# Convolution layer and pooling layer in one block, with the pooling done by banded matrices on TensorE

## What is computed

```
# odd layer (h = modulated RMS norm of x)
bg, cg, xt, g = split(h @ odd_w_in, 4)            # 1024 -> 4 x 1024
conv = three-tap convolution of cg * xt along positions
x = x + gate * ((bg * conv * silu(g)) @ odd_w_out)

# pooling layer
h = x * rsqrt(mean(x*x, channels) + eps) * norm_mix_g
for each of 4 groups of 256 channels, windows w = 2, 4, 8, 16:
    d = (mean of the last w positions of h, fewer at the start) - h
    y = d @ pool_w[group] + pool_b                # 256 x 256 per group
x = x + pool_scale * y
```

## Time and profile before

| quantity | value |
|---|---|
| time, median of 3 runs | 2083.51 us (2082.96 to 2085.34) |
| span of the profiled execution | 2083.1 us |
| TensorE matmul busy | 1915.1 us, 92% |
| VectorE busy | 1061.5 us, 51% |
| ScalarE busy | 621.8 us, 30% |
| GpSimd busy | 474.6 us, 23% |
| mean HBM traffic | 60 GB/s |

### The profile page before, as it was taken

The page is one execution under the profiler, slowest core; times in us unless marked ns, Lnnn a source line. Parts: engine busy times, 40 slices in busy tenths (PEclk is TensorE's granted clock), DMA queues, the critical chain, the costliest instruction groups (busy, mean ns, idle before and its releaser), DMA issues. The chain is left out here.

```text
span 2083.1 us, 24691 instructions
## 1 busy us (share of the span) xinstructions
PE 1915.1 (92%) x9917; PEld 1611.9 (77%) x9917; DVE 1061.5 (51%) x1007; ACT 621.8 (30%) x815; POOL 474.6 (23%) x200
## 2 busy tenths in 40 slices
PE   5799999889996989999999964699999999999998
PEld 3799988668885867888888853578888888888886
DVE  3633662468886325333333379744544535445454
ACT  4312211556665213222212032422222222222222
POOL 0211211000000212322222126222323233232221
PEclk9899999999998989999999986799999999999999
DMA  7311112800001412111111000111102111020212
GB/s 289 128 41 41 48 51 66 334 23 1 0 0 61 162 35 57 51 51 51 50 50 50 10 21 0 51 59 32 60 30 60 39 52 60 30 60 30 60 40 81
DMA packets 132701, 125.90 MB, mean 60 GB/s; under 512 B 6510, under 2 KB 118695, under 8 KB 131495
## 3 DMA queue, kind: packets, MB, share of 16 engines
q1 hardware_dynamic: 132647, 125.12, 18.8%
HBM read 113.57 MB, written 11.53 MB: 60 GB/s over the span
## 5 line engine op out<-in xcount | busy, mean ns | idle before, releaser
L2009 DVE TENSOR_TENSOR residual<-ps,residual 128x1024 f32<-128x1024 f32 x176 | 215.1, 1224 | 199.5 <-PE ps L106 199.2
L628 PE MATMUL ps<-in_hi,h_hi 128*128 128x256 f32 x512 | 145.7, 285 | 9.1 <-DVE h_lo L194 9.1
L628 PE MATMUL ps<-in_lo,h_hi 128*128 128x256 f32 x512 | 145.5, 284 | 0.0
L628 PE MATMUL ps<-in_hi,h_lo 128*128 128x256 f32 x512 | 145.5, 284 | 0.0
L1931 ACT ACTIVATE branches<-ps,cols 128x1024 f32<-128x1024 f32 x44 | 53.1, 1207 | 271.4 <-PE ps L106 264.8
L1994 DVE SCALAR_TENSOR_TENSOR branches<-ps,cols,branches 128x1023 f32<-128x1023 f32 x44 | 56.2, 1278 | 141.7 <-ACT branches L1931 141.7
L122 POOL TENSOR_TENSOR in_lo<-in_raw,in_hi 128x2048 fp32r<-128x2048 f32 (+1 forms) x16 | 59.4, 3715 | 287.2 <-ACT in_hi L119 233.7
L1647 DVE SCALAR_TENSOR_TENSOR residual<-ps,ada_col,residual 128x1024 f32<-128x1024 f32 x64 | 81.6, 1282 | 81.6 <-PE ps L106 77.5
L106 PE MATMUL ps<-yf_hi,f_hi 128*128 128x512 f32 x336 | 105.8, 396 | 1.1 <-DVE residual L2009 1.1
L106 PE MATMUL ps<-h_hi,hi_va 128*128 128x512 f32 x336 | 104.3, 392 | 2.6 <-DVE branches L1997 2.6
L628 PEld LDWEIGHTS ps<-in_hi,h_hi 128*128 128x128 f32 x512 | 99.0, 193 | 9.5 <-issue 9.5
(11 more groups left out here) (354 smaller groups left out, 4398.7 us busy)
## 6 DMA issues: line engine op xcount, KB each, us to landing
ada_raw_rest<-in_ada_w SPq DMA_DIRECT2D x32, 512.0 KB, 6.1
raw_va<-in_ffn_w_in SPq DMA_DIRECT2D x22, 512.0 KB, 5.5
raw_ga<-in_ffn_w_in SPq DMA_DIRECT2D x22, 512.0 KB, 6.4
f_raw<-in_ffn_w_out SPq DMA_DIRECT2D x22, 512.0 KB, 3.6
ada_raw<-in_ada_w SPq DMA_DIRECT2D x8, 1024.0 KB, 18.9
in_raw<-in_even_w_in SPq DMA_DIRECT2D x8, 1024.0 KB, 5.2
residual<-in_x SPq DMA_DIRECT2D x2, 2048.0 KB, 10.7
x_scratch<-fq SPq DMA_DIRECT2D x8, 512.0 KB, 6.1
```

Source lines behind the costliest of these rows:

```text
L628: last = pe.matmul(ps[:, n % 8, 0:HALF_GROUP], x[:, k, r * P:(r + 1) * P], w[:, u % 2, k, :], start=(k == 0 and x is hi and w is w_hi), st ...
L2009: dve.tensor_tensor(res[:, d, :], pair[DOWN_PAIR[d]], res[:, d, :], ALU.add)\
```

## The change

The block `pool` is gone, and its work stands in the block `odd`. It uses that the norm is one number per position and the projection runs over channels, so the two can be exchanged.

- **Weights.** `norm_mix_g` is multiplied into the pooling weights (`pool_weights`, ScalarE). They are loaded into the buffers `raw_cg` and `raw_xt` of the odd layer once those are free, and split as before.
- **Projection of the raw residual.** `res` tiles are split into `h1_hi` and `h1_lo` when they are final (`high`, `x_low`). `z_group(r, g)` then makes the rows of position block r, group g: six products of 256 columns, where the x tile is the stationary operand, so that the result lies with positions on partitions. Position blocks 0 to 2 run ahead of the mean of squares, blocks 3 to 7 behind it.
- **Norm.** The square sum stands in the odd block. Its root and reciprocal are applied as one scale per partition when the result is copied out of PSUM (`z_high` on ScalarE, `z_low` on VectorE). The eight transposes (L210) of the pooling layer are gone.
- **Pooling.** `banded(m)` multiplies each position block of z with a matrix of 128 by 144 that holds window mean minus identity. Per channel tile m there are 16 products of 144 or 128 columns and three of 16. The matrices are made by VectorE (`window_ones`, before the first step of the odd layer) and GpSimd (`bands`, after the last one).
- **End.** `pool_add`, bias and the square sum for the ffn norm are as before, with other buffers.

```diff
+                        def z_group(r, g):
+                            out = pair[Z_PAIR[r % 4]][:, g * HALF_GROUP:(g + 1) * HALF_GROUP]
+                            for t in (2 * g, 2 * g + 1):
+                                for x, w in ((h1_hi, hi), (h1_hi, lo), (h1_lo, hi)):
+                                    last = pe.matmul(out, x[:, t, r * P:(r + 1) * P], pool_weight(w, t),
...
+                        def banded(m):
+                            g, out, cs = m // 2, pair[Z_PAIR[m % 4]], slice(m * P, (m + 1) * P)
+                            for b in range(RT):
+                                if m == 0:
+                                    pe.wait_ge(sem("z_low"), b + 1)
...
                         down(N - 1, N, (last_d_hi, last_d_lo, last_y_hi, last_y_lo))
-                        squares.tensor(pe)
...
+                        pe.wait_ge(sem("pw_low"), 2)
+                        for g in range(4):
+                            x_low_stands(pe, 2 * g)
+                            x_low_stands(pe, 2 * g + 1)
+                            for r in range(3):
+                                if g == 0 and r:
+                                    res_final(pe, 4 + r)
+                                last = z_group(r, g)
...
+                        for p, (name, tiles) in enumerate((("x_summed_pool", SUM_ON_POOL), ("x_summed_dve", SUM_ON_VECTOR))):
+                            pe.wait_ge(sem(name), len(tiles))
...
+                        for r in range(3, RT):
+                            if r == 3:
+                                pe.wait_ge(sem("x_rooted"), 1)
+                            else:
+                                pe.wait_ge(sem("z_low"), r - 3)
...
+                        for m in range(KT):
+                            if m >= 4:
+                                pe.wait_ge(sem("pool_added"), m - 3)
+                            else:
+                                pe.wait_ge(sem("z_low"), 5 + m)
+                            banded(m)
                         squares.tensor(pe)
```

More of the change, by code:

```diff
@@ L1597, in _ @@
                         last_rest()
-                        for d in squares.ON_POOL:
-                            squares.add(pool, d)
+                        bands()
+                        for i, k in enumerate(kinds[0:2]):
+                            pool.wait_ge(sem("pw_high"), i + 1)
+                            split_low(pool, lo[k][:, :, :], raw[k][:, :, :], hi[k][:, :, :], sem("pw_low"))
+                        for d in LOW_ON_POOL:
+                            pool.wait_ge(sem("x_high"), d + 1)
+                            split_low(pool, h1_lo[:, d, :], res[:, d, :], h1_hi[:, d, :], sem("x_low_pool"))
+                        for i, m in enumerate(SUM_ON_POOL):
+                            pool.wait_ge(sem("x_squared"), m + 1)
+                            if i:
+                                pool.wait_ge(sem("x_summed_pool"), i)
+                            pool.tensor_tensor(square_totals[0], square_totals[0], square_of[m], ALU.add)\
+                                .then_inc(sem("x_summed_pool"), 1)
+                        for m in squares.ON_POOL:
+                            squares.add(pool, m)
                     @block.vector
@@ L1666, in _ @@
                         add(N - 2, tiles=range(2, KT))
-                        add(N - 1, squared=True)
+                        add(N - 1, tiles=range(0, 5))
+                        x_low(2)
+                        add(N - 1, tiles=range(5, 7))
+                        x_low(6)
+                        add(N - 1, tiles=range(7, 8))
+                        x_low(7)
+                        for i, m in enumerate(SUM_ON_VECTOR):
+                            dve.wait_ge(sem("x_squared"), m + 1)
+                            if i:
+                                dve.wait_ge(sem("x_summed_dve"), i)
+                            dve.tensor_tensor(square_totals[1], square_totals[1], square_of[m], ALU.add)\
+                               .then_inc(sem("x_summed_dve"), 1)
+                        dve.wait_ge(sem("x_rooted"), 1)
+                        dve.reciprocal(compact[:, :], compact[:, :]).then_inc(sem("x_inverse"), 1)
+                        dve.wait_ge(sem("x_inverse"), 1)
+                        for r in range(RT):
+                            dve.wait_ge(sem("z_high"), r + 1)
+                            dve.scalar_tensor_tensor(out=z_lo[:, r, :], in0=pair[Z_PAIR[r % 4]], scalar=compact[:, r:r + 1],
+                                                     in1=z_hi[:, r, :].bitcast(F32), op0=ALU.mult, op1=ALU.subtract)\
+                               .then_inc(sem("z_low"), 1)
+                        for m in range(KT):
+                            pool_add(m)
+                            if m - 1 in squares.ON_VECTOR:
+                                squares.add(dve, m - 1)
+                        squares.add(dve, KT - 1)
                     @block.tensor
@@ new lines, in _ @@
+                        res_final(pe, KT - 1)
+                        for p, (name, tiles) in enumerate((("x_summed_pool", SUM_ON_POOL), ("x_summed_dve", SUM_ON_VECTOR))):
+                            pe.wait_ge(sem(name), len(tiles))
+                            for r in range(RT):
+                                last = pe.matmul(ps[:, 7, r:r + 1], square_totals[p][:, r * P:(r + 1) * P], ones[:, 0:1],
+                                                 start=(p == 0 and r == 0), stop=(p == 1 and r == RT - 1))
```

347 lines of the change are left out of this document (182 added, 165 removed).

## The result

| | before | after |
|---|---|---|
| median of 4 runs each | 2083.24 us | 2070.36 us (2068.69 to 2071.73) |
| ratio, with its 95% interval | | 0.9938 (0.9924 to 0.9952) |
| profiled execution: time, span | 2083.51, 2083.1 us | 2071.73, 2070.0 us |
| end of the last down product of the odd layer | 1225.8 | 1232.8 |
| from there to the square root of the ffn layer | 96.4 us | 77.0 us |

The account below looks back on a forecast made before the run. VectorE and GpSimd bound the 96.4 us before the ffn layer, TensorE everything else. Steps 1 to 5 put the ffn root at 1292.3 instead of 1322.2: 29.9 off 2083.5 gives 2054 us, range 2046 to 2072.

Parts of the forecast that it names:

- Costed at nothing: Odd layer: `window_ones` fits into 8.8 us of VectorE idle time and the weight load comes early enough; no cost.
- If the steps of the odd layer change in length: A sign named in advance that the prediction is wrong; no size given.
- Step 1: Odd block, until the mean of squares: last square addition ends near 1245 us; projection of blocks 0 to 2 hides.
- Steps 2 and 3: Norm done by 1249.0 us, then projection blocks 3 to 7, partly at half clock; last low part by 1268.3.
- Step 4: Banded products: 135 not hidden, at 0.112 us each with the clock holding, 15.1 us, ending at 1283.4.
- Step 5: From the last banded product to the ffn root: 4.5 plus 4.4 us, root at 1292.3.
- Rival 2: Narrow banded products cost double, 0.223 to 0.25 us, or run at 1.2 GHz: 2068 to 2072 us; chance 0.25.
- Rival 3: Early projection blocks do not hide (2063 us), or blocks 3 to 7 stay at 1.2 GHz (2064); chance 0.10.
- rival 4: Slower than before: narrow products at float32 price and 1.2 GHz, some 0.45 us each, 2105 us; chance 0.05.

Follow-up runs that it names:

- The padding: The changed kernel with 32 unused bytes per partition ahead of `yo_hi` in the odd layer: 2062.84 us, ratio to before 0.9896.
- the one with the moved pause: The changed kernel with TensorE waiting for the last `z_low` ahead of the first banded product instead of ahead of block 7 of the first result: 2075.18 us.

## Why the prediction was off

The forecast had the ffn root at 1292.3 and it came at 1309.75, 17.4 us later. By the prediction's own steps, each from its start:

- **Costed at nothing: the odd layer. +7.0, of which 5.7 are the change.** The other 1.3 stood there before the layer began, and are chance. The prediction looked there for idle time that hides `window_ones` and for the place of the weight load in SP's queue, and both were right: the load was issued at 1172.70, and nobody waited for it. What it passed over is that the diff moves buffers. "If the steps of the odd layer change in length" stood among the things that would prove it wrong, but nothing in the working asked where the operands of those steps now lie. The padding takes 6.7 us off the layer without touching an instruction.
- **Step 1, the square sum. -0.8.** The fourth square addition ended at 1251.17, 18.4 us behind the last down product, against 19.2. The turns beside a busy GpSimd were dearer (2.68 and 3.18 for the first two additions), the low parts cheaper (1.23 for the last). The projection of the blocks 0 to 2 hid, as forecast.
- **Steps 2 and 3. 0.** The root stood 22.0 us behind the last down product (23.2 forecast), the last `z_low` ended 41.7 behind (42.5), so the 0.8 of step 1 was all that was gained. The half clock at the head of the burst was there, 5 us of it.
- **Step 4, the banded products. +11.6.** At 2.4 GHz the price of 0.112 us was right as a mean: the second result came in 2.12 us for 19 products, 0.1116 each. That is in part luck. The step assumed one distance whatever the products stream, but in the rows above a start follows 0.11 to 0.12 behind a product of 144 columns and 0.08 behind one of 16, and the two errors cancel. The sentence that failed is "the clock should hold, since a stretch of 20 us made mostly of 128-column records stood at 1.00". That stretch was mixed, with products of 256 and 512 columns for some 40% of its time, and so no evidence for a stream that has narrow ones alone. The step also gave no weight to the pause that step 3 had put there itself: "then the last copy and low part, 2.3". The experiments show that it takes both: narrow products alone held the clock at 1.00 for 17 us, a pause of 0.53 us with wide products behind it did too, and the two together lost it. From 1277.24 on the distance was 0.213, so that the step took 26.7 instead of 15.1 us.
- **Step 5. -0.4.** 8.55 us from the last product to the root, against 8.9.

Sum: 7.0 - 0.8 + 11.6 - 0.4 = 17.4. Behind the root the kernel is 0.7 us shorter than before; that was not forecast, and no run here says why. The experiment that shifts bg and gt in the kernel before, whose code and buffers behind that root are those of the kernel before, has 759.7 us there against 760.9, so the 0.7 is no more than the difference of two executions.

Rival 2 named the time: 2068 to 2072, "the same time comes if they run at 1.2 GHz, with 0.22". Its way was half right: the 1.2 GHz was there. But it had the whole loss in step 4, and in the measured kernel 7.0 of it lie ahead of the first projection, so that it met 2070 is luck. Its other ground, narrow products that cost double at full clock, did not happen (0.112). Rival 3 did not happen: the early blocks hid, and blocks 3 to 7 were at full clock after 5 us. Nor did rival 4: a narrow product at 1.2 GHz costs 0.213, not 0.45.

The Trainium skill (TensorE: Matmul & The Clock Gate, "Step-by-step: what each phase is for") says that the weights of the next product and the moving data of the current one come through two read ports of their own, so that loading weights takes nothing from a running product. The runs here don't fit it without a remark: at a distance of 0 modulo 256 between weights and moving data the products are 0.2267 us apart, at 32 they are 0.2333, with the same instructions. No run shows that it is the reading of the weights that costs the difference.

The same page ("HAM oscillation — how this bites in real kernels") puts a lowered clock down to waits of TensorE between bursts, longer ones than the 0.67 us here. The trace agrees with half of it: without the wait the clock held. It leaves out that a wait of 0.53 us did no harm where the products behind it had 256 columns, and that narrow ones stayed at 1.2 GHz for 32.5 us without a gap.

Two things stay open. Why the distance of the addresses counts: the runs show its size and its period, not its cause. And how long a pause narrow products stand: 0.67 us was too much in the changed kernel, with none the clock held, and nothing between was run.

## What to carry to other kernels

A change that adds, splits or reorders buffers can change the length of products whose code it doesn't touch: list the addresses of weights and moving operands in both builds and compare their distances, before the trace is read. Here small or odd-sized buffers ahead of an operand cost 5.7 to 6.7 us (the odd layer of the changed kernel) and some 7 of the 9 us measured (`compact3`, in the kernel before), and placing them behind the operand costs nothing. And where a stream of narrow products is laid behind a wait, price it at the lower clock too, or put the wait where wide products follow it, or put other work of the stream into it.

## What was not expected of the hardware

- 512-column F32R products with the weights and the moving operand 32 bytes apart modulo 256 start 0.2333 us apart instead of 0.2267 (2.9% more); 64 apart, 0.2289, and 256 apart 0.2267 again; shown in both directions, in two layers, with kernels between 2074 and 2095 us that differ from the kernel before in unused bytes or allocation order alone.
- TensorE busy all the time doesn't mean 2.4 GHz: 24.0 us at a granted 0.50 in the changed kernel and 32.5 us in the one with the moved pause, both with the array and the weight load busy for 100% of the stretch.
- One result of 19 narrow F32R products (144, 128 and 16 columns, each with weights of its own) takes 2.12 us at 2.4 GHz and 4.05 at 1.2, in the mean 0.112 and 0.213 us per product; a product of 256 columns in the projection 0.120 and 0.214. Widened to 256 columns, a result takes 2.25 us instead of 2.12, which was worth it only through the clock.
